# Direct term of the last mixer's state scan: added after the next step's rotation instead of right behind its own pair

## The reference, cut to what matters

```python
bu_re = jnp.einsum('gph,sbgh->sbgp', bb_re, ut)      # input product, and the same for bu_im
_, _, x_re, x_im = lax.associative_scan(_s5_combine, (a_re, a_im, bu_re, bu_im), axis=0)
y = (jnp.einsum('ghp,sbgp->bsgh', c_re, x_re) - jnp.einsum('ghp,sbgp->bsgh', c_im, x_im)
     + d_skip * ug)                                   # d_skip * ug is the direct term
y = jax.nn.gelu(y.reshape(B, S, S5_WIDTH))
return y * jax.nn.sigmoid(y @ w_glu + b_glu)
```

## Time and profile before

| | us |
|---|---|
| median of three runs | 3178.13 (3174.97 to 3179.16) |
| the profiled execution | 3178.93 |
| its span, first to last instruction | 3177.6 |
| TensorE busy in the span | 3063.5 |
| VectorE busy in the span | 2136.1 |
| mean granted TensorE clock | 0.99 |

### The profile page before, as it was taken

One profiled execution on the slowest core, in us unless ns is written; L12 is line 12 of the kernel. 1 busy time (PEld: TensorE's weight loads), 2 busy tenths in 40 slices (PEclk: granted clock), 3 DMA queues, 4 the chain that ended last, 5 costly groups with the idle time before them and its releaser, 6 DMA issues. The chain is left out here.

```text
span 3177.6 us, 58106 instructions
## 1 busy us (share of the span) xinstructions
PE 3063.5 (96%) x26070; PEld 2609.7 (82%) x26094; DVE 2136.1 (67%) x1978; ACT 1447.6 (46%) x1362; POOL 675.0 (21%) x752
## 2 busy tenths in 40 slices
PE   8999899999999999999999999999999999899987
PEld 7888788888888888578888888887686888666876
DVE  6767777777757566557777877565485554886654
ACT  4443555444434544665555555444454543113542
POOL 3555145445465200000300000000310000112300
PEclk9999999999999999999999999999999999999999
DMA  9888488888898555444766666653545454554343
GB/s 339 301 301 305 164 279 305 308 298 299 310 319 294 189 178 180 155 169 142 256 226 219 232 223 213 235 207 102 197 147 192 167 178 172 193 200 148 133 146 106
DMA packets 305785, 693.30 MB, mean 218 GB/s; under 512 B 16240, under 2 KB 20464, under 8 KB 299520
## 3 DMA queue, kind: packets, MB, share of 16 engines
q1 hardware_dynamic: 269952, 564.22, 51.4%
q0 software_dynamic: 35584, 125.36, 11.0%
HBM read 625.56 MB, written 63.96 MB: 217 GB/s over the span
## 5 line engine op out<-in xcount | busy, mean ns | idle before, releaser
L596 PE MATMUL PSG<-XH,WS 128*128 128x256 bf16 x11296 | 1880.5, 274 | 28.5 <-DVE WS L1573 13.6
L1573 DVE TENSOR_TENSOR WS<-WF,WS 128x2048 bf16<-128x2048 f32 (+1 forms) x487 | 1197.3, 2482 | 620.7 <-ACT WS L1078 620.3
L596 PE MATMUL PSG<-XL,WS 128*128 128x256 bf16 x5648 | 1545.5, 274 | 0.0
L596 PEld LDWEIGHTS PSG<-XH,WS 128*128 128x128 bf16 x11296 | 1109.6, 98 | 175.2 <-issue 36.5
L1078 ACT ACTIVATE WS<-WF 128x2048 bf16<-128x2048 f32 (+1 forms) x487 | 913.3, 1899 | 630.1 <-PE PSG L596 258.1
L596 PE MATMUL PSG<-SCR,WS 128*128 128x256 bf16 x6720 | 746.0, 273 | 3.6 <-DVE SCR L2094 3.6
L596 PEld LDWEIGHTS PSG<-SCR,WS 128*128 128x128 bf16 x6720 | 659.6, 98 | 86.4 <-issue 3.9
L596 PEld LDWEIGHTS PSG<-XL,WS 128*128 128x128 bf16 x5648 | 554.6, 98 | 67.7 <-issue 0.3
L513 POOL TENSOR_TENSOR SCR<-SCR 128x1024 bf16<-128x1024 f32 x92 | 235.3, 2558 | 3.4 <-DMA weight_halves<-SCR 1.8
L596 PE MATMUL PB<-SCR 128*128 128x128 f32 (+3 forms) x928 | 155.2, 330 | 34.4 <-DVE SCR L2175 18.4
L596 PE MATMUL PSG<-WS,XH 128*128 128x512 bf16 x620 | 186.9, 380 | 1.5 <-issue 0.9
(11 more groups left out here) (243 smaller groups left out, 1728.8 us busy)
## 6 DMA issues: line engine op xcount, KB each, us to landing
WF<-ffn_w_up SPq DMA_DIRECT2D x176, 1024.0 KB, 6.5
WF<-ffn_w_down SPq DMA_DIRECT2D x88, 1024.0 KB, 6.5
WF<-ab_w_in SPq DMA_DIRECT2D x56, 1024.0 KB, 5.2
WF<-a_w_in SPq DMA_DIRECT2D x48, 1024.0 KB, 7.9
weight_halves<-SCR POOLq DMA_DIRECT2D x184, 256.0 KB, 5.8
WS<-weight_halves SPq DMA_DIRECT2D x46, 1024.0 KB, 4.8
SCR<-cd_w_in POOLq DMA_DIRECT2D x80, 512.0 KB, 6.8
WF<-a_w_out SPq DMA_DIRECT2D x16, 1024.0 KB, 7.1
```

What stands on the lines that cost most here:

```text
L596: return nc.tensor.matmul(o, lhsT, rhs, start=start, stop=stop, skip_group_check=True)
L1573: tt(l, w, h, ALU.subtract).then_inc(s_lo, 1)
```

## The change

The direct term is put into a helper. For the pairs 0 to 6 it is issued in the first step of the next pair, behind that step's four rotation instructions and in front of the yield and the scans. For pair 7 it is issued behind the loop. The number of yields is the same. The instructions, their operands and the two semaphores are the same; each wait moves with its instruction.

```diff
+                def add_direct(j):
+                    nc.vector.wait_ge(s_yb, 2 * j + 2)
+                    stt(U[:, j, :], U[:, j, :], pr("s5_d", j), PB[:, 2, 0:T], ALU.mult, ALU.add).then_inc(s_ty, 1)
+
                 yield
                 for n in range(16):
                     j = n // 2
...
                     tt(V1[:, 0, :, :], V1[:, 0, :, :], V2[:, 1, :, :], ALU.add)
                     t = own.mark(tt(V1[:, 1, :, :], V1[:, 1, :, :], V2[:, 0, :, :], ALU.subtract))
+                    if n and n % 2 == 0:
+                        add_direct(j - 1)
                     yield
...
                     yield
                     if n % 2:
                         yield
-                        nc.vector.wait_ge(s_yb, n + 1)
-                        stt(U[:, j, :], U[:, j, :], pr("s5_d", j), PB[:, 2, 0:T], ALU.mult, ALU.add).then_inc(s_ty, 1)
-                    yield
+                    yield
+                add_direct(7)
                 for g in range(2):
```

## The result

The changed kernel takes 3159.41 us (median, 3157.82 to 3161.77) against 3178.64 of the kernel before: ratio 0.9937, 95% interval 0.9925 to 0.995. A second set of runs on the same chip as the last experiments gave 3160.67 against 3179.05, ratio 0.9945 (0.9932 to 0.9959). The profiled execution took 3157.82, its span is 3156.5 us. In the changed kernel L2158 and L2159 are the first two instructions of the rotation, L2162 its last, L2147 the direct term, L2171 the scans, L2181 the last instruction of a state.

A forecast was written before the change was run, and what follows sets the result against it. TensorE bounds the whole kernel; in the scan it and VectorE, nearly equally loaded, run in step. Last state 15.8 us earlier plus 1.6 of clock gives 17.4: 3178.9 - 17.4 = 3161.5, forecast 3161, range 3155 to 3169.

The forecast's parts named there:

- The cause, two engines that wait for each other at each pair's end: In the scan, TensorE waits 18.4 us for VectorE's state and VectorE 19.3 us at the direct term for TensorE.
- Waits removed, 15.9 us: VectorE's idle time at the direct terms: 4 x 2.09 + 2.92 + 4.57 us go; the last, 3.48, stays.
- The scans of step 9 held by 1.5 us by a late output product 8: In the new order TensorE is late at output product 8, and VectorE's scans of step 9 wait 1.5 us.
- The direct term costs the same in both places: zero: On VectorE, its 0.40 us moves from before the rotation to behind it; the state-to-state distance keeps it, so zero added.
- The clock behind the last output product, 1.6 us: The low-clock loss of 1.6 us on TensorE at the scan's end should go, its wait being 1.2 instead of 2.69.
- only the wait at input product 7 would keep a low stretch: TensorE's wait behind the FF scan stays, about 4.6 us, the only one as long as those followed by low clock.
- Behind the scan nothing changes: After the last output product the lists stay the same, so the 17.4 us gain carries over in full.
- The 11 us that the prediction puts as lost to the clock there: Behind the scan, granted clock 0.96 means some 11 us lost, whose places can shift by a few us.
- Rival 1: In the scan, TensorE becomes the bound and its clock doesn't recover: gain 11.7 us, time 3167; chance 0.20.
- Rival 2: Gain given back by stages behind the scan, or engine order not changed as said: 3172 to 3179 us; chance 0.07.
- Rival 3: The load of the next pair's output weights comes late and TensorE waits at seven pairs: 3185 us; chance 0.03.
- whether loads would slip by an instruction: GpSimd's loads, issued while VectorE is never idle, could slip by one VectorE instruction; no cost if the slack holds.

The follow-up runs named there:

- e1: Against the kernel before, the direct term moved behind the next rotation for pairs 5 and 6 only; 3169.9 us, ratio 0.9971.
- e2: Against the kernel before, the direct term moved behind the next rotation for pairs 0 to 4 only; 3169.2 us, ratio 0.9972.
- e8: The changed kernel with the load of each pair's output weights issued twice, one behind the other, and waited for twice; 3180.3 us, one run.
- e5: The kernel before with unused matmuls put in front of TensorE's four long waits; 3176.1 us, ratio 0.9989.
- e6: The changed kernel with 40 unused matmuls in front of input product 7 only; 3160.8 us, one run.

## Why the prediction was right

Forecast 3161 (gain 17.4), range 3155 to 3169; measured 3159.4 and 3160.7, a gain of 18 to 19.

- *The cause, two engines that wait for each other at each pair's end.* Shown by e1 and e2: the two halves add up to the whole within 0.6 us, though each missed its own S (by 1.3 and 2.4 us), both times beside a low stretch of another length than before.
- *Waits removed, 15.9 us.* VectorE's idle time at the direct terms fell by 17.2 us, 1.4 of it at the last, which I had left at 3.48 and which is 2.09: the output product there now runs at the full clock. That is 15.8 for the six that were to go (the prediction calls five of them plain, but lists and sums all six).
- *The scans of step 9 held by 1.5 us by a late output product 8.* Measured 1.89, and 0.20 at step 7.
- *The direct term costs the same in both places: zero.* This term was mis-sized. It costs 0.48 in the old place (0.40 at pair 2) and 0.22 in the new one: six times 0.26 and once 0.18, 1.7 us of gain that I hadn't counted. The sum of S: 15.85 of waits, 1.12 and 0.38 of waits at the second fd group and the scans of step 5 that went, less 2.09 of new ones, plus 1.7: 17.0, and 188.4 - 171.3 = 17.1 was measured. I had 15.8 for it.
- *The clock behind the last output product, 1.6 us.* Measured 3.39 - 1.99 = 1.4. The mean granted clock in the scan rose from 0.96 to 0.98; that only the wait at input product 7 would keep a low stretch was right, and its wait, forecast at 4.6 us, was 4.62. The wait of 1.68 at output product 4, of which I didn't know on which side it lay, kept the full clock.
- *Behind the scan nothing changes.* 283.74 against 283.82. The 11 us that the prediction puts as lost to the clock there is 0.04 of the whole stretch, TensorE's 31.6 us of idle time counted in; it is too high, and it entered the range only.
- *Rival 1* (TensorE becomes the bound, the clock stays low) fell: VectorE's waits at the scans are 2.1 us, under the 4 that would have shown it. *Rival 2* fell with the stretch behind. *Rival 3* did not happen; e8 shows what it would have cost. The prediction also asked whether loads would slip by an instruction. The Trainium skill, SBUF — State Buffer, section "SBUF: two separate sides", says that GpSimd can't write the descriptors of such a load while VectorE runs an instruction in a two-port mode. The median landing of the output weights went from 5.0 to 5.4 us and that of the rotation factors from 5.0 to 4.4, so no slip of a whole 1.2 us instruction can be seen; whether the instructions here hold the shared ports at all, no run tests.

The two profiled executions differ by 21.1 us, 2.7 more than the scan explains. That lies ahead of the scan in code that is the same: the granted clock from 2500 us to the first rotation was 0.97 in one and 0.99 in the other. Taken at face value it would have made the change look better than it is.

## What to carry to other kernels

Where an engine consumes what another has just made from its own last result, look whether it has work that needs neither, and put the consumer behind that; the wait costs on both engines, and, where it is long, the clock behind it. Write out both engines' orders with measured durations before moving it: here that gave S within 1.5 us, told which wait would stay, and pointed to the next gain. When the second engine then has idle time in front of the first, give it more of its own independent work there, but check the next wait too: with two steps more the wait moved on by one product and took 2 of the 5 us along, with three it was gone. That is by F; only the kernel with six steps more is told from the changed one by its times.

## What the runs showed of the hardware

- Two VectorE instructions of this scan overlap by 0.08 us where the second needs nothing of the first. The scans start 0.10 us after the rotation that they wait for; the other instructions of a step that wait for the one before them start 0.03 to 0.04 after it (L2161 above). An independent instruction put in between costs less than its duration: 0.22 of 0.47 us and 0.01 of 0.15 in front of the scans, 0.26 of 0.46 behind them.
- Behind the waits of TensorE of 2.69 to 4.62 us in this stretch the granted clock fell to its lower level for 3.4 to 6.9 us, with one exception; behind waits of 1.72 us and less it stayed at 1.00. The exception is the wait of 2.81 us in e8 at output product 10, longer than the one of 2.69 before, behind which it fell. So the length of the wait alone doesn't decide whether the clock falls. Nor does it set for how long: behind the same wait at output product 4 the clock was low for 6.8 us before and for 3.5 in e1. No run here tests what decides it. The window behind the exception:

```profile
2838.38:2842.00 3.62, 3.62 (x25) 3.14 (x26) 1.52 (x2) 0.00 (x0) 0.00 (x0) 1.00 0.27 111
```

- Matmuls that nobody needs, put in place of the long waits, kept the clock at 1.00 (e5, e6).
- The same code ahead of the scan took up to 5.9 us more or less from one profiled execution to another (first rotation 2699.0 to 2704.9). A length inside the trace tells a change of 2 us that the total time doesn't.
